# Retention stage: decayed queries made after the transpose, normalisation one turn later

## What is computed

```python
# per tile (chunk), per head, in both directions
a     = (q @ k.T) * intra                  # intra: decay^(i-j), masked
o     = a @ v + (q @ s) * q_dec            # q_dec = decay^(pos+1)
s_new = s * c_dec + (k * k_dec).T @ v      # k_dec = decay^(127-pos)
# both directions are added, then normalised over a head's columns and gated
o   = (o - mean(o)) * rsqrt(var(o) + EPS) * gn_w
ret = silu(g) * o
```

## Time and profile before

| | us |
|---|---|
| median of 3 runs (lowest, highest) | 3613.22 (3609.57, 3617.61) |
| the profiled execution's own time | 3617.4 |
| its span in the profile | 3615.6 |
| retention stage in it | about 740 to 837 |
| mean granted PE clock, as a share | 0.979 |

### The profile page before, as it was taken

One profiled execution on the slowest core, in us unless ns is written; L12 is line 12 of the kernel. 1 busy time (PEld: TensorE's weight loads), 2 busy tenths in 40 slices (PEclk: granted clock), 3 DMA queues, 4 the chain that ended last, 5 costly groups with the idle time before them and its releaser, 6 DMA issues.

```text
span 3615.6 us, 55127 instructions
## 1 busy us (share of the span) xinstructions
PE 3446.7 (95%) x18150; PEld 2870.8 (79%) x18150; DVE 2974.9 (82%) x5746; ACT 1386.0 (38%) x2092; POOL 1478.6 (41%) x1125
## 2 busy tenths in 40 slices
PE   7899889987999979999999999999999999999998
PEld 2899769876444446788898889899888999999976
DVE  8455678864698999799999999988898998888987
ACT  7411454452122228534444444433333333333332
POOL 3223120042322210264444444464466766566653
PEclk9999999998999989999999999999999999999999
DMA  8699429855411128999999999999999999999997
GB/s 308 210 359 352 151 92 321 301 203 191 152 35 35 64 96 317 326 342 352 344 359 352 336 351 352 353 358 365 308 356 379 371 376 365 369 361 371 370 327 263
DMA packets 399666, 1047.91 MB, mean 290 GB/s; under 512 B 32106, under 2 KB 185550, under 8 KB 390194
## 3 DMA queue, kind: packets, MB, share of 16 engines
q0 software_dynamic: 134416, 505.99, 39.2%
q1 hardware_dynamic: 217068, 482.75, 36.6%
q10 hardware_dynamic: 48056, 57.70, 4.6%
HBM read 892.52 MB, written 153.80 MB: 289 GB/s over the span
## 4 chain that ended last, share of the span: by engine, by line
PE 54%; DMA 4%; DVE 2%; issue 1%; POOL 1%; ACT 0%; SPq 0%; DVEq 0%; ACTq 0%
PE p_y L2833 26%; PE p_a L2816 8%; PE p_a L2815 8%; PE p_a L2819 8%; PE pw L2228 2%; DMA weights_spill<-wt 1%; PE p_y L2790 1%; DMA rows<-in_v,pairsT 1%; DMA v_raw<-in_v 1%; DVE h_rows L2703 1%; POOL rows L2565 0%; DVE rows L2688 0%; DMA rows<-u_rows,pairsT 0%; DMA x1g<-h_spill 0%; DMA u_raw<-in_v 0%
## 5 line engine op out<-in xcount | busy, mean ns | idle before, releaser
L2565 POOL DMA_INDIRECT rows<-u_rows,pairsT x384 | 487.5, 1270 | 587.0 <-DVE pairsT L2688 536.6
L2565 POOL DMA_INDIRECT rows<-in_v,pairsT x384 | 584.5, 1522 | 345.3 <-DVE h_rows L2703 262.5
L2815 PE MATMUL p_a<-h_hi,u_hi 128*128 128x384 f32 x1856 | 624.5, 336 | 5.5 <-ACT pairsT L2515 4.6
L2816 PE MATMUL p_a<-h_lo,u_hi 128*128 128x384 f32 x1856 | 627.6, 338 | 0.0
L2703 DVE SCALAR_TENSOR_TENSOR h_rows<-rows,pairsT,h_rows 128x1024 f32<-128x1024 f32 x381 | 475.9, 1278 | 41.2 <-DMA rows<-in_v,pairsT 40.9
L2688 DVE CUSTOM_DVE_ANT_0 rows<-rows,h_rows 128x1024 f32<-128x1024 f32 x384 | 458.6, 1217 | 18.8 <-DMA rows<-u_rows,pairsT 18.6
L2833 PE MATMUL p_y<-v_hi,g_hi 128*128 128x512 f32 x1464 | 466.3, 400 | 6.6 <-ACT g_hi L2521 6.6
L2833 PE MATMUL p_y<-v_lo,g_hi 128*128 128x512 f32 x1464 | 455.4, 392 | 0.0
L2833 PE MATMUL p_y<-v_hi,g_lo 128*128 128x512 f32 x1464 | 373.3, 390 | 4.2 <-DVE g_lo L2681 4.2
L2819 PE MATMUL p_a<-h_hi,u_lo 128*128 128x384 f32 x1856 | 360.4, 335 | 5.4 <-DVE u_lo L2647 5.4
L2815 PEld LDWEIGHTS p_a<-h_hi,u_hi 128*128 128x128 f32 x1856 | 350.3, 189 | 16.0 <-issue 5.9
(11 more groups left out here) (382 smaller groups left out, 6046.8 us busy)
## 6 DMA issues: line engine op xcount, KB each, us to landing
v_raw<-in_v SPq DMA_DIRECT2D x244, 512.0 KB, 6.5
u_raw<-in_uT SPq DMA_DIRECT2D x232, 512.0 KB, 7.3
w_ring<-weights_spill POOLq DMA_DIRECT2D x31, 1536.0 KB, 14.9
wada<-in_w_ada SPq DMA_DIRECT2D x48, 512.0 KB, 7.0
u_rows<-pairsT ACTq DMA_DIRECT2D x48, 512.0 KB, 7.2
key_cols<-in_uT SPq DMA_DIRECT2D x48, 512.0 KB, 7.3
u_rows<-key_rows SPq DMA_DIRECT2D x48, 512.0 KB, 6.0
weights_spill<-wt SPq DMA_DIRECT2D x24, 1024.0 KB, 5.0
```

What stands on the lines that cost most here:

```text
L2565: pool.indirect_dma_start(rows[s][n % SLOTS][:], None, (keep.u_rows, v_rows)[g], at).then_inc(rows_in[s][n % SLOTS], 16)
L2815: nc.tensor.matmul(p_a[:, 0:GT], u_hi[s][:, k, :], h_hi[:, k, :], start=k == 0, stop=False)
L2816: nc.tensor.matmul(p_a[:, 0:GT], u_hi[s][:, k, :], h_lo[:, k, :], start=False, stop=False)
```

## The change

`queries(t)` on POOL no longer reads the loaded slot: it multiplies the turned queries `qT` (ACT's copy) with two new tiles of decays, and writes `qfT` and `qbT` directly. The decays are made once, at the head of the stage, by two instructions of DVE (steps) and eight Exp of ACT. The transposes of the decayed queries (PE), the copy of qfT (ACT) and of qbT (DVE) are gone, and so are two banks; one of them becomes a third `bank_o`. `decayed_keys` moves from DVE to ACT (four instructions, one for each head, behind `sigmoid`). On DVE the statistics of a tile come ahead of its state, and root, normalisation and gate product of a tile come one turn later: `turn(t)` ends with `normalised(t - 1)`, ACT's `turn(t)` has `deviation(t - 1)`.

```diff
@@ POOL @@
             def queries(t):
                 if t >= TILES:
                     return
-                pool.wait_ge(z_in[t % SLOTS], t // SLOTS * 16 + 16)
-                wait_count(pool, t2_full, t)
-                decayed(qf[:], zt[t % SLOTS][:, 0], 0).then_inc(qf_full, 1)
-                decayed(qb[:], zt[t % SLOTS][:, 0], 1).then_inc(qb_full, 1)
+                pool.wait_ge(query_decays_full, 1)
+                pool.wait_ge(qT_full, t + 1)
+                wait_count(pool, o_full, t - 1)
+                nc.gpsimd.tensor_mul(qfT[t % 2][:], qT[:], query_decays[:, 0]).then_inc(qfT_full, 1)
+                nc.gpsimd.tensor_mul(qbT[t % 2][:], qT[:], query_decays[:, 1]).then_inc(qbT_full, 1)
...
             def turn(t):
-                queries(t + 2)
+                if t >= 0:
+                    queries(t + 1)
                 gate(t + 1)
@@ PE, turned(t) and result(t) @@
-                pe.wait_ge(qf_full, t + 1)
-                pe.wait_ge(qb_full, t + 1)
-                wait_count(pe, qfT_full, t)
-                wait_count(pe, qbT_full, t)
-                for h in range(HEADS):
-                    nc.tensor.transpose(bank_qf[:, h, :], qf[:, h, :], keep.ident)
-                for h in range(HEADS):
-                    last = nc.tensor.transpose(bank_qb[:, h, :], qb[:, h, :], keep.ident)
-                last.then_inc(t2_full, 1)
...
-                wait_count(pe, on_full, t - 1)
+                wait_count(pe, on_full, t - BANKS + 1)
@@ ACT @@
+            act.wait_ge(steps_full, 2)
+            for n in range(8):
+                last = nc.scalar.activation(query_decays[:, n // 4, n % 4, :], query_steps[:, n // 4, :], ACT.Exp, scale=keep.log_decay[:, n:n + 1])
+            last.then_inc(query_decays_full, 1)
 
             def copies(t):
                 if t >= TILES:
                     return
                 act.wait_ge(t1_full, t + 1)
                 wait_count(act, a_full, t)
+                wait_count(act, qfT_full, t)
+                wait_count(act, qbT_full, t)
                 nc.scalar.activation(qT[:], bank_q[:], ACT.Copy).then_inc(qT_full, 1)
                 nc.scalar.activation(kT[:], bank_k[:], ACT.Copy).then_inc(kT_full, 1)
-                act.wait_ge(t2_full, t + 1)
-                wait_count(act, o_full, t - 1)
-                nc.scalar.activation(qfT[t % 2][:], bank_qf[:], ACT.Copy).then_inc(qfT_full, 1)
+
+            def decayed_keys(t):
+                if t >= TILES:
+                    return
+                act.wait_ge(z_in[t % SLOTS], t // SLOTS * 16 + 16)
+                wait_count(act, st_full, t - 2)
+                for h in range(HEADS):
+                    last = nc.scalar.activation(kf[t % 3][:, h, :], zt[t % SLOTS][:, 1, h, :], ACT.Copy, scale=keep.dec[:, 2, h:h + 1])
+                last.then_inc(kf_full, 1)
...
+            def deviation(t):
+                if t < 0:
+                    return
+                act.wait_ge(var_full, t + 1)
+                wait_count(act, rec_full, t)
+                nc.scalar.activation(rs[:, 0, :], mv[t % 2][:, :, 1], ACT.Sqrt, bias=keep.cols[:, 4:5]).then_inc(std_full, 1)
+
             def turn(t):
-                if t >= 0:
-                    copies(t + 1)
-                    act.wait_ge(var_full, t + 1)
-                    nc.scalar.activation(rs[:, 0, :], mv[:, :, 1], ACT.Sqrt, bias=keep.cols[:, 4:5]).then_inc(std_full, 1)
-                    sigmoid(t + 2)
-                else:
-                    sigmoid(0)
-                    sigmoid(1)
+                if t < 0:
+                    for n in range(2):
+                        sigmoid(n)
+                        decayed_keys(n)
+                    return
+                copies(t + 1)
+                deviation(t - 1)
+                sigmoid(t + 2)
+                decayed_keys(t + 2)
...
             order(keep_mixed, copies, turn)
+            deviation(TILES - 1)
@@ DVE @@
+            nc.vector.tensor_scalar(query_steps[:, 0], keep.grid[:, C_IOTA, :], 1.0, None, ALU.add).then_inc(steps_full, 1)
+            nc.vector.tensor_scalar(query_steps[:, 1], keep.grid[:, C_IOTA, :], -1.0, float(P), ALU.mult, ALU.add).then_inc(steps_full, 1)
             dve.wait_ge(keep.ret_in, 64)
...
             def turn(t):
                 if t < 0:
                     masked(0)
-                    decayed_keys(0)
-                    decayed_keys(1)
-                    return
-                copy(t + 1)
-                state(t)
+                    return
                 dve.wait_ge(o_full, t + 1)
                 wait_count(dve, var_full, t)
                 for h in range(HEADS):
-                    last = nc.vector.bn_stats(stats[:, h, :], bank_o[t % 2][:, h, :])
+                    last = nc.vector.bn_stats(stats[:, h, :], bank_o[t % BANKS][:, h, :])
                 last.then_inc(stats_full, 1)
+                state(t)
+                masked(t + 1)
                 dve.wait_ge(stats_full, t + 1)
-                wait_count(dve, on_full, t)
+                wait_count(dve, on_full, t - 1)
                 dve.sem_inc(waited, 1)
                 for h in range(HEADS):
-                    last = nc.vector.bn_aggr(mv[:, h, :], stats[:, h, :])
+                    last = nc.vector.bn_aggr(mv[t % 2][:, h, :], stats[:, h, :])
                 last.then_inc(var_full, 1)
-                masked(t + 1)
-                decayed_keys(t + 2)
+                normalised(t - 1)
+
+            def normalised(t):
+                if t < 0:
+                    return
                 dve.wait_ge(std_full, t + 1)
...
             order(chain, early, turn)
+            normalised(TILES - 1)
```

More of the change, by code:

```diff
@@ L1284, in stage_retention @@
     zt = [m.sb(f"zt{i}", [P, 4, HEADS, P]) for i in range(SLOTS)]
-    qf = m.sb("qf", [P, HEADS, P])
-    qb = m.sb("qb", [P, HEADS, P])
+    query_steps = m.sb("query_steps", [P, 2, P])
+    query_decays = m.sb("query_decays", [P, 2, HEADS, P])
     kf = [m.sb(f"kf{i}", [P, HEADS, P]) for i in range(3)]
@@ L1297, in stage_retention @@
     stats = m.sb("stats", [P, HEADS, 6])
-    mv = m.sb("mv", [P, HEADS, 2])
+    mv = [m.sb(f"mv{i}", [P, HEADS, 2]) for i in range(2)]
     rs = m.sb("rs", [P, 2, HEADS])
     on = m.sb("on", [P, HEADS, P])
-    bank_q, bank_k, bank_qf, bank_qb, bank_a, bank_s = (
-        m.ps(f"bank_{x}", [P, HEADS, P]) for x in ("q", "k", "qf", "qb", "a", "s"))
-    bank_o = [m.ps(f"bank_o{i}", [P, HEADS, P]) for i in range(2)]
+    bank_q, bank_k, bank_a, bank_s = (m.ps(f"bank_{x}", [P, HEADS, P]) for x in ("q", "k", "a", "s"))
+    BANKS = 3
+    bank_o = [m.ps(f"bank_o{i}", [P, HEADS, P]) for i in range(BANKS)]
     s_in, g_in, z_in = sem("s_in"), sem("g_in"), [sem(f"z_in{i}") for i in range(SLOTS)]
@@ L1307, in stage_retention @@
     kb_full, sb_upd, sb_next = sem("kb_full"), sem("sb_upd"), sem("sb_next")
[L1308 to L1311, removed]
+    kf_full, qT_full, kT_full, qfT_full, qbT_full = (sem(x) for x in ("kf_full", "ret_qT", "ret_kT", "ret_qfT", "ret_qbT"))
+    steps_full, query_decays_full = sem("query_steps_full"), sem("query_decays_full")
+    t1_full, a_full, aT_full, o_full, st_full, sf_next, sig_full, sg_full = (
+        sem(x) for x in ("ret_t1", "ret_a", "ret_aT", "ret_o", "ret_st", "sf_next", "gate_sig", "gate_silu"))
     decays_full, waited = sem("decays_full"), sem("aggr_waited")
@@ L1470, in result @@
                     v = slice(h * P, (h + 1) * P)
-                    last = nc.tensor.matmul(bank_o[t % 2][:, h, :], aT[t % 2][:, h, :], z[:, 2, h, :], start=True, stop=prompt)
+                    last = nc.tensor.matmul(bank_o[t % BANKS][:, h, :], aT[t % 2][:, h, :], z[:, 2, h, :], start=True, stop=prompt)
                     if not prompt:
-                        nc.tensor.matmul(bank_o[t % 2][:, h, :], qfT[t % 2][:, h, :], s_f[:, v], start=False, stop=False)
+                        nc.tensor.matmul(bank_o[t % BANKS][:, h, :], qfT[t % 2][:, h, :], s_f[:, v], start=False, stop=False)
                         back = keep.state_early if t == TILES - 1 else s_b[:, t]
-                        last = nc.tensor.matmul(bank_o[t % 2][:, h, :], qbT[t % 2][:, h, :], back[:, v], start=False, stop=True)
+                        last = nc.tensor.matmul(bank_o[t % BANKS][:, h, :], qbT[t % 2][:, h, :], back[:, v], start=False, stop=True)
                 last.then_inc(o_full, 1)
@@ L1563, in masks @@
                 dve.wait_ge(mask_full, 2)
-            def decayed_keys(t):
-                if t >= TILES:
-                    return
[L1568 to L1577, removed]
             def masked(t):
@@ L1587, in early @@
                 masks()
-                copy(t)
             def state(t):
@@ L1631, in turn @@
                 for h in range(HEADS):
-                    last = nc.vector.tensor_scalar(on[:, h, :], bank_o[t % 2][:, h, :], mv[:, h, 0:1], rs[:, 1, h:h + 1], ALU.subtract, ALU.mult)
```

(1 more changed line is left out.)

## The result

| | before | after |
|---|---|---|
| median of 3 runs, us (lowest, highest) | 3613.22 (3609.57, 3617.61) | 3638.17 (3634.08, 3638.93) |
| profiled execution: span, us | 3615.6 | 3636.0 |
| mean granted PE clock | 0.979 | 0.977 |
| retention stage, POOL's first to DVE's last instruction, us | 95.2 | 110.6 |
| step 3 of the chain, from the stage's start, us | 12.4 | 15.5 |

The kernel became slower: ratio 1.0055, 95% interval 1.004 to 1.007. The forecast was +5.4 us; measured are +25 in the medians, and the stage alone is 15.4 longer.

A forecast was written before the change was run, and what follows sets the result against it. The prediction took the stage's turns as bound by DVE's work, 7.03 us, and after the change by a ring of waits. +1.4 + 5.4 - 1.4 = +5.4 us on the 3613.2 median gave 3618.6 us, range 3610 to 3630.

The forecast's parts named there:

- The sum: Retention stage: +1.4 up to weights(2), +5.4 for six turns, -1.4 after them, +5.4 us in all; bounds -1.4 to +8.1.
- the verdict "same": Whole kernel: measured time not told from no change, about 0.2% or 7.2 us; chance 0.63.
- What joins them: Prediction's section on the waits linking engines in a turn: floor 7.14 us, with both table loads over near 3.95.
- the ring: Closed chain of waits through copies, weights, masked, aggregate, normalised, sigmoid and decayed keys, once a turn; forecast 8.1 us.
- POOL's hold: In each turn, DVE's gate product stands until POOL's second gate product is over, ending 0.55 later, at 6.30 us.
- the third rival: In the turns, sigmoid's wait is met in time and ACT sets 5.75 us a turn; 3605.5 us, chance 0.05.
- a mere slowing: In the turns, POOL's product only slows DVE's gate product, to 1.25 us, instead of holding it; turn 7.7 us.
- The first rival: In the turns, POOL is not in the gate product's way; turn 7.14 us, sum +0.7, 3613.9 us, chance 0.20.
- The head: Stage's start: chain step 3 delayed by POOL's queries(0), +3.2 to 3.6 us, leaving +1.4 at weights(2).
- The six turns: From weights(2) to weights(8): first turn 7.1, five at 8.1, 47.6 against 42.16 us, so +5.4.
- The tail: From weights(8) to the stage's end: 11.9 us, or 13.5 at PE's lower clock, against 14.1; taken as -1.4.
- The second rival: In the turns, gaps keep PE at its lower clock; turn 10.1 us, +16, 3629 us, chance 0.13.

The follow-up runs named there:

- e1_swap: Changed kernel with the two waits ahead of the sigmoid exchanged, the one for the gate product first; median 3624.13 us, ratio 1.0026 to the kernel before.
- e3_keys_dve: Changed kernel with the decayed keys moved from ACT back to the end of DVE's turn; median 3623.28 us, ratio 1.0017 to the kernel before.
- e5_short_gate: e1_swap with POOL's second gate product cut to 8 of its 512 columns; median 3619.18 us, ratio 1.0006 to the kernel before.
- e2_sigmoid_late: Changed kernel with ACT's sigmoid one turn later, sigmoid(t + 1) instead of sigmoid(t + 2); median 3608.18 us, ratio 0.9982 to the kernel before.
- e6_late_q0: Changed kernel with ACT's sigmoid one turn later and POOL's queries(0) after the backward chain; median 3602.60 us, ratio 0.9966 to the kernel before.

## Why the prediction was wrong

**The sum was +5.4 us, the stage gave +15.4, the medians +20 to +25.** The side was right, the case and the size were not: 3638.17 lies outside 3610 to 3630, and the verdict "same" held most of the chance.

**The step that failed** is one sentence in "What joins them": that the two table loads are over by 3.95, ahead of the sigmoid's wait. I took the load for work that fits into the idle time because in the profile before it always did: the sigmoid's load stood at 789.48 with its wait met, and the root's load at 785.90 ran ahead of the one wait that the root has. After the change the sigmoid's load itself waits: it starts 0.08 or 0.09 behind the gate product in every turn, and its 1.29 us lie in the ring. e1_swap took them out with the exchange of two lines. Six turns of 1.29 are 7.7 of the 10 us that the stage came out above the forecast, and with the load out of the ring the stage is 5.9 us over the kernel before, near the sum's +5.4.

**The ring** was right: copies, `weights`, `masked`, aggregate, normalised, sigmoid, decayed keys. Its forecast of 8.1 is e1_swap's 8.06; less the decayed keys it loses what they take (e3_keys_dve); less POOL's hold it is 7.23 for 7.14 (e5_short_gate); opened, the turn is 5.65, for which the third rival had 5.75 with ACT as the bound (e2_sigmoid_late). **POOL's hold** was right as well, 6.32 for 6.30; the reading as a mere slowing, 7.7, was wrong. Where the product is held, POOL's four products set the length of the ring, and not the leg over `weights` and `masked`: in the turn shown they end 5.77 from the start of `copies`, and the gate product 0.55 later. The first rival (POOL not in the way) hung on 0.19 us between the start of POOL's product and the readiness of DVE's; in the turn shown it was 0.29 (804.57 to 804.86).

**The head** was near: step 3 of the chain 3.1 later for the forecast 3.5, the clock low in that step as feared (2.07), and at `weights(2)` +1.1 for +1.4. The forecast's own terms, 3.2 to 3.6 with 0.3 more and 2.5 less, give 1.0 to 1.4, so the sum took their upper end.

**The six turns**: the forecast was 7.1 + 5 x 8.1 = 47.6. Measured 55.7, of which 7.7 is the load. The rest, 0.4, lies in part in the first of them, which took 7.29 in e1_swap for the forecast 7.1, and in part in the turns of the lower clock.

**The tail** was taken at -1.4 and came at +0.7. Its full-speed term, 11.9 from `weights(8)`, is near what e1_swap (12.06), e5_short_gate (12.06) and e6_late_q0 (11.66) show. In the changed kernel PE ran the last `result` at the lower clock, 5.3 us instead of 2.8, after idle times of 2.18 and 1.27 us on either side of `weights(8)`; in e1_swap these were 0.67 and 1.28, and the clock stayed at its full level. The bound of 13.5 allowed 1.6 us for that clock; it took 2.8.

**The second rival**, the lower clock, did not set the turn: its sign, products of PE at up to twice their length, was there in some turns, its turn of 10.1 us in none. The clock did fall: 0.88 of full speed over the six turns, and `weights` took from 1.06 to 2.05. Here is the turn in which it took longest, on PE and DVE:

```profile
810.62 2.05 PE L1448 MATMUL bank_a<-qT,kT 128*128 128x128 f32 x8 [3.18 <-ACT qT L1510]
...
812.70 0.69 DVE L1586 TENSOR_TENSOR aT<-bank_a,decay_T 128x512 f32<-128x512 f32 x1 [4.11 <-PE bank_a L1448]
...
815.18 0.69 DVE L1638 TENSOR_TENSOR mix<-on,sg 128x512 f32<-128x512 f32 x1
```

`masked` comes 0.9 us late, and the gate product starts late, at 815.18, when POOL's is all but over (813.97 to 815.24), and takes 0.69. It ends at 815.87, 6.40 from the start of `copies` where the turn above had 6.32. That turn was 9.49 us long, the other late ones 9.40 or 9.41: nearly all the time that the slow clock costs is time the product would have stood.

## What to carry to other kernels

When a wait that was always met comes to bind, ask which instruction carries it. An activation that needs a table load is two instructions, and a load that looked hidden joins the path if the binding wait sits on it; the order of two waits in the source decided 1.3 us a turn here. When a stage is put off by a turn, look for the buffers that it frees: here three gate buffers and a sigmoid made two turns ahead closed a ring through four engines, and moving the sigmoid by one turn made a change that lost 20 us into one that gains 7, and 13 with the head repaired.

## What was not expected of the hardware

With two waits ahead of an activation that needs a table, the load took the second one in the source and the activation the first: idle time of 3.74 us ahead of the load in the changed kernel, of 2.39 behind it once the waits were exchanged. With the root's one wait, before the change, the activation took it and the load ran ahead (1.98 us idle between them).

POOL's product of two dense 128x512 tiles takes 1.27 us, the one with a broadcast operand 1.04; the forecast had taken the first from the gate's row, and the new queries show 1.26 to 1.27 in the turns of the changed kernel. POOL's product is held in its turn when DVE's starts first. In the six turns of e2_sigmoid_late DVE's gate product began 0.03 to 0.19 ahead of POOL's first product and took 0.69 to 0.78; POOL's took 1.72 to 1.78 instead of 1.27 and ended 1.12 to 1.14 behind DVE's end. One of them:

```profile
798.91 0.69 DVE L1638 TENSOR_TENSOR mix<-on,sg 128x512 f32<-128x512 f32 x1
...
799.02 1.72 POOL L1389 TENSOR_TENSOR qfT<-qT,query_decays 128x512 f32<-128x512 f32 x1
```
